# Order of the 64x64 products of a recurrence on TensorE: one half of the rows after the other, or the two halves in turn

## The chip, the cores and the metric

The kernel runs on one core of one Trainium2 chip. The metric is the device time of one execution in microseconds (us), lower is better. The kernel before was executed three times for its time; the median is 2512.82 us (2508.73 to 2514.59).

## The reference, cut to what matters

The reference is one layer of a decoder trunk: 256 tokens, 2048 channels, everything in float32. It has a token mixer of four parallel branches, a cross-attention into 256 memory tokens and a gated MLP. The change touches only one branch of the mixer, the RWKV-7 recurrence over 8 heads of 64 channels:

```python
def step(state, inp):
    r_t, w_t, k_t, v_t, kk_t, a_t = inp
    sa = jnp.einsum('bhvk,bhk->bhv', state, -kk_t)
    state = (state * w_t[:, :, None, :]
             + sa[..., None] * (kk_t * a_t)[:, :, None, :]
             + v_t[..., None] * k_t[:, :, None, :])
    return state, jnp.einsum('bhvk,bhk->bhv', state, r_t)
```

The projections around it (`z = h @ w_in` and the others) are large products of 128x128 weight tiles with 256 tokens.

## The kernel before, in words

**The recurrence in chunks.** The 256 steps are cut into 4 chunks of 64 tokens. In a chunk the recurrence becomes a set of 64x64 matrices per head: products of the scaled operands (the stages `rw_s1` to `rw_s4`), the inverse of a triangular matrix by five doubling levels (`rw_level`, `rw_level2`), and then, chunk by chunk, the right-hand side, the solution, the state and the output (`rw_chunk_a`, `_b`, `_c`).

**Where the matrices lie.** 8 heads by 4 chunks are 32 matrices of 64x64. Two heads share the 128 partitions: one head in partitions 0 to 63, the other in 64 to 127. So there are 16 positions `g` along the free axis, times 2 halves `h`. A product takes its two operands from one half of the partitions and writes its result to the same half of PSUM, so it uses 64 rows and 64 columns of TensorE's array: half 0 the one quarter, half 1 the quarter diagonally opposite.

**How a product becomes instructions.** Every float32 product of this kernel that isn't split by hand is two matmul instructions in the profile, each with a weight load of its own. A call of `pe.matmul` in these stages is thus two instructions on PE and two on PEld.

**The two helpers of the change.** `per_head` (L438) calls a product for all 16 positions of half 0 and then for all 16 of half 1: 32 products, 64 instructions. It is called 20 times (once in `rw_s1`, `rw_s2` and each of five `rw_level`; twice in `rw_s3`, `rw_s4` and in `rw_level2` of the levels 1 to 4; once in `rw_level2` of level 5). All these products are recorded under L452. In `rw_s1` and `rw_s2` a product has 128 columns, elsewhere 64. `four` (L525) does the same for the 4 positions of one chunk, where a result may be the sum of two or three products; its products are recorded under L531. It is called 15 times, for 224 products.

**PSUM.** `small_mm` puts position `g` at bank `base + g // 8` for 64 columns and `base + g // 4` for 128. `four` puts position `i` at bank `base + i // 2`.

**The order around it.** TensorE's queue is written out by hand: the list `MIX` holds the projections (`project`, L390, its matmuls under L396; those of the compressed keys under L615), and the dictionary `steps` (L742) says which recurrence stage is issued ahead of which projection. A projection is 16 products, or 32 instructions, and the burst of small products stands between two of them. VectorE and ScalarE evict the results of a burst (`rw_level`'s by L1671, which is `masked` at L1648, and L1673 and L1676) while TensorE does the next projection. The weights of a projection (1 MB) come through a ring of 4 slots, filled by SyncE (L326) once a slot has been used.

Of the kernel before, what the change touches and what calls it, by code (L numbers as in the profile page):

```python
# [139 lines left out]
def program(nc, A, const_dram, decay_dram, const_at, out):  # L140
# [4 lines left out]
    with ctx:  # L145
# [61 lines left out]
        sm = ctx.enter_context(nc.psum_tensor("sm", [P, 6, 512], f32))  # L207
# [174 lines left out]
        def _(pe):  # L382
# [55 lines left out]
            def per_head(fn):  # L438

                for h in range(2):
                    for g in range(16):
                        mm = fn(slice(64 * h, 64 * h + 64), g)
                return mm

            def b64(base, g, w=64):
# [42 lines left out]
            def rw_s1():  # L489
                pe.wait_ge(sem("rw_operands"), 1)  # L490
                pe.wait_ge(sem("rw_bonus_out"), 1)
                per_head(lambda r, g: small_mm(0, r, g, G["B"][r, g], QR[r, g, :, :], w=128)) \
                    .then_inc(sem("rw_s1_mm"), 1)

            def rw_s2():
                pe.wait_ge(sem("rw_s1_out"), 1)
                per_head(lambda r, g: small_mm(0, r, g, G["C"][r, g], QR[r, g, :, :], w=128)) \
                    .then_inc(sem("rw_s2_mm"), 1)

            def rw_s3():  # L500
                pe.wait_ge(sem("rw_s2_out"), 1)
                per_head(lambda r, g: small_mm(0, r, g, QR[r, g, 0, :], G["B"][r, g])).then_inc(sem("rw_s3_mm"), 1)
                per_head(lambda r, g: small_mm(2, r, g, G["Vc"][r, g], eye(r))).then_inc(sem("rw_s3_mm"), 1)
# [19 lines left out]
                        .then_inc(sem("rw_p2_mm"), 1)  # L523

            def four(base, off, fn):  # L525
                for h in range(2):
                    r = slice(64 * h, 64 * h + 64)
                    for i in range(4):
                        pairs = fn(r, i)
                        for q, (a, b) in enumerate(pairs):  # L530
                            mm = pe.matmul(sm[r, base + i // 2, off + i % 2 * 64:off + i % 2 * 64 + 64], a, b,  # L531
                                           start=q == 0, stop=q == len(pairs) - 1)
                return mm

            v4 = lambda a: a.rearrange("p (i t) -> p i t", t=64)
# [2 lines left out]
            def rw_chunk_a(c):  # L538

                if c == 0:  # L540
                    pe.wait_ge(sem("rw_x_ready"), 6)
                else:
                    pe.wait_ge(sem("rw_state"), c)
                    pe.wait_ge(sem("rw_y_out"), c)
                four(0, 0, lambda r, i: ([(QR[r, 4 * i + c, 0, :], S4[r, i])] if c else [])
                     + [(G["L2"][r, 4 * i + c], G["V"][r, 4 * i + c])]).then_inc(sem("rw_rhs_mm"), 1)

            def rw_chunk_b(c):

                pe.wait_ge(sem("rw_rhs_out"), c + 1)  # L550
                four(2, 0, lambda r, i: [(G["X"][r, 4 * i + c], X04[r, i])]).then_inc(sem("rw_u_mm"), 1)

            def rw_chunk_c(c):

                pe.wait_ge(sem("rw_u_out"), c + 1)
                if c < NCH - 1:
                    four(2, 128, lambda r, i: [(G["Bt"][r, 4 * i + c], U4[r, i]),
                                               (G["Ct"][r, 4 * i + c], G["V"][r, 4 * i + c])]) \
                        .then_inc(sem("rw_ds_mm"), 1)
                four(0, 128, lambda r, i: ([(S4[r, i], QR[r, 4 * i + c, 1, :])] if c else [])  # L560
                     + [(U4[r, i], G["M1"][r, 4 * i + c]), (G["V"][r, 4 * i + c], G["M2"][r, 4 * i + c])]) \
                    .then_inc(sem("rw_y_mm"), 1)
# [1587 lines left out]
```

## Time and profile before

| what | value |
|---|---|
| median of three executions | 2512.82 us |
| fastest, slowest | 2508.73, 2514.59 us |
| span of the profiled execution | 2503.8 us |
| median less span | 9.0 us |
| PE busy | 2398.1 us (96%), 14320 instructions |
| PEld busy | 2085.0 us (83%), 14320 instructions |
| DVE, ACT, POOL busy | 1384.9, 1045.6, 236.1 us |
| HBM read | 389.34 MB, 156 GB/s over the span |

The profile is one profiled execution. Its span runs from the first to the last recorded instruction; the listing has no separate total for it, so its own time is taken as the span and the 9.0 us that the median of the three executions lies above it. PE is TensorE's matmul, PEld its weight load, DVE is VectorE, ACT is ScalarE. The recorded duration of a matmul reaches from its start to a modelled end, and matmuls overlap in the pipeline, so the pace of a stream is read from its starts or from the length of the whole stream divided by its count, not from the mean duration.

### The profile page before, as it was taken

How to read it: one execution, taken by the hardware profiler on the slowest of the kernel's cores; microseconds unless marked ns; L12 is line 12 of the kernel's file. 1: busy time of each engine (PE TensorE's matmuls, PEld its weight loads, DVE VectorE, ACT ScalarE, POOL GpSimd, SP SyncE). 2: the span in 40 equal slices, each digit the busy share in tenths (PEclk: the TensorE clock that was granted, in tenths of full speed). 3: DMA queues.
4: the chain of work that ended last, by engine and by line, in shares of the span. 5: the costliest groups of instructions: out<-in, count | busy, mean ns of one | idle time of the engine just before them, and what ended most of it. 6: DMA issues, size and time to landing. Idle time of an engine off the chain costs nothing.

```text
span 2503.8 us, 38637 instructions
## 1 busy us (share of the span) xinstructions
PE 2398.1 (96%) x14320; PEld 2085.0 (83%) x14320; DVE 1384.9 (55%) x1676; ACT 1045.6 (42%) x1463; POOL 236.1 (9%) x240
## 2 busy tenths in 40 slices
PE   5989999999999999999999999896999999999996
PEld 4869989789888888887887888785888888888885
DVE  5661110221118666666677544356877777776665
ACT  4320001112114555555444444345655555555553
POOL 0120100000000000000421000031111111111110
PEclk9989997999999999999999999998999999999998
DMA  6512222233334555556555554252655555555663
GB/s 224 185 51 85 98 102 78 97 133 113 124 118 152 185 187 186 189 189 212 194 171 165 181 173 153 93 188 86 198 186 186 184 182 188 189 163 188 186 185 127
DMA packets 104459, 392.77 MB, mean 157 GB/s; under 512 B 11600, under 2 KB 20048, under 8 KB 94000
## 3 DMA queue, kind: packets, MB, share of 16 engines
q1 hardware_dynamic: 104080, 390.31, 47.2%
q8 instruction: 67, 1.10, 0.2%
q10 hardware_dynamic: 288, 1.17, 0.1%
q14 instruction: 24, 0.20, 0.0%
HBM read 389.34 MB, written 2.10 MB: 156 GB/s over the span
## 4 chain that ended last, share of the span: by engine, by line
PE 73%; issue 18%; DVE 6%; ACT 1%; POOL 1%; DMA 0%; DVEq 0%; POOLq 0%; ACTq 0%
PE bank L797 29%; PE bank L800 15%; PE bank L396 13%; PE sm L452 3%; PE bank L414 2%; PE bank L426 2%; PE sm L531 1%; PE bank L417 1%; PE bank L615 1%; DVE part L1876 1%; DVE part L1970 1%; DVE part L1539 1%; PE sm L905 1%; PE sm L435 1%; PE sm L887 1%
## 5 line engine op out<-in xcount | busy, mean ns | idle before, releaser
L797 PE MATMUL bank<-part,part 128*128 128x512 f32 x4224 | 1488.4, 399 | 35.1 <-issue 16.3
L800 PE MATMUL bank<-part,part 128*128 128x256 f32 x4224 | 1150.6, 282 | 0.0
L1876 DVE TENSOR_TENSOR part<-part,part 128x1024 fp32r<-128x1024 f32 (+1 forms) x632 | 795.0, 1268 | 370.7 <-ACT part L1139 358.4
L797 PEld LDWEIGHTS bank<-part,part 128*128 128x128 f32 x4224 | 783.8, 189 | 212.0 <-issue 20.1
L800 PEld LDWEIGHTS bank<-part,part 128*128 128x128 f32 x4224 | 799.7, 189 | 21.5
L1139 ACT ACTIVATE part<-part 128x1024 fp32r<-128x1024 f32 (+1 forms) x632 | 662.8, 1050 | 349.7 <-PE bank L800 320.9
L396 PE MATMUL bank<-part,part 128*128 128x256 f32 (+1 forms) x1632 | 364.3, 383 | 0.0
L396 PEld LDWEIGHTS bank<-part,part 128*128 128x128 f32 (+1 forms) x1632 | 307.4, 190 | 50.0 <-issue 5.1
L1213 ACT ACTIVATE part<-bank 128x256 f32<-128x256 f32 x236 | 90.3, 382 | 291.1 <-PE bank L797 291.1
L992 ACT ACTIVATE part<-bank 128x256 f32<-128x256 f32 (+1 forms) x59 | 22.7, 384 | 413.3 <-PE bank L396 375.5
L1884 DVE TENSOR_TENSOR part<-bank,part 128x256 f32<-128x256 f32 (+1 forms) x236 | 99.8, 423 | 132.9 <-ACT part L1213 132.8
L1476 POOL TENSOR_TENSOR part<-part 128x256 f32 (+1 forms) x48 | 48.1, 1003 | 763.2 <-DVE part L1884 763.2
L797 PE MATMUL sm<-part,part 128*128 128x512 f32 x320 | 110.8, 397 | 1.3 <-DVE part L1890 0.7
L414 PE MATMUL bank<-part,part 128*128 128x512 f32 x256 | 90.9, 403 | 8.7 <-DVE part L1575 8.7
L800 PE MATMUL sm<-part,part 128*128 128x256 f32 x320 | 79.4, 281 | 0.0
L452 PEld LDWEIGHTS sm<-part 64*64 64x64 f32 x1088 | 71.6, 139 | 7.6 <-issue 7.6
L452 PE MATMUL sm<-part 64*64 64x64 f32 (+1 forms) x1088 | 73.7, 233 | 2.1 <-DVE part L1639 2.1
L1501 POOL TENSOR_TENSOR part<-part 128x256 f32<-128x256 f32 x44 | 32.5, 738 | 424.1 <-DVE part L2051 424.1
L417 PE MATMUL bank<-part,part 128*128 128x256 f32 x256 | 69.8, 283 | 0.0
L797 PEld LDWEIGHTS sm<-part,part 128*128 128x128 f32 x320 | 56.8, 188 | 11.0 <-DVE part L1890 1.5
L800 PEld LDWEIGHTS sm<-part,part 128*128 128x128 f32 x320 | 60.1, 188 | 5.8
L414 PEld LDWEIGHTS bank<-part,part 128*128 128x128 f32 x256 | 47.7, 190 | 20.4 <-issue 9.7
(304 smaller groups left out, 1576.0 us busy)
## 6 DMA issues: line engine op xcount, KB each, us to landing
part<-in_w_up SPq DMA_DIRECT2D x176, 512.0 KB, 4.5
part<-in_w_g SPq DMA_DIRECT2D x104, 512.0 KB, 4.2
part<-in_w_dn SPq DMA_DIRECT2D x64, 512.0 KB, 3.5
part<-in_w_out SPq DMA_DIRECT2D x32, 512.0 KB, 4.0
part<-in_w_mk SPq DMA_DIRECT2D x32, 512.0 KB, 4.3
part<-in_w_mv SPq DMA_DIRECT2D x32, 512.0 KB, 3.9
part<-in_w_q SPq DMA_DIRECT2D x32, 512.0 KB, 3.8
part<-in_w_o SPq DMA_DIRECT2D x32, 512.0 KB, 3.9
```

The lines of the kernel that those rows point to most:

```text
L396: mm = pe.matmul(big[0:M, n % 2, 0:rhs_n], w[:, k * M:(k + 1) * M], x[:, k, :], start=k == 0, stop=k == KT - 1)
L414: mm = pe.matmul(b, w[:, 0, k, :], x, start=h == 0 and k == 0, stop=last, skip_group_check=True)
L417: mm = pe.matmul(b[:, T:2 * T], w[:, 1, k, :], x[:, 0:T], start=False, stop=False, skip_group_check=True)
L426: mm = pe.matmul(dst[:, s * P:(s + 1) * P], x[:, k, s * P:(s + 1) * P], ring[:, n % NSLOT, k, :], start=k == 0, stop=k == KT - 1)
L452: return pe.matmul(sm[rows, b, c:c + w], lhsT, rhs, start=start, stop=stop)
L797: mm = pe.matmul(dst, w[:, 0, k, :], x[:, k0 + k, :], start=start and k == 0, stop=last, skip_group_check=True)
L800: mm = pe.matmul(dst[:, T:2 * T], w[:, 1, k, :], x[:, k0 + k, 0:T], start=False, stop=False, skip_group_check=True)
L1139: act.activation(wsplit[(2 * m + h) % 4][:, 0, 0:n, :], raw[:, m % 2, h, 0:n, :], cp) .then_inc(sem("hi_done"), 1)
L1213: act.activation(cross[:, b, :], bank[:, b, T:2 * T], cp).then_inc(sem("cross_out"), 1)
L1476: pool.tensor_tensor(sq[:, n % 2:n % 2 + 1, :], tile, tile, MUL).then_inc(sem("y_sq"), 1)
L1876: tt(w[:, 1, 0:n, :], raw[:, m % 2, h, 0:n, :], w[:, 0, 0:n, :].bitcast(f32), SUB).then_inc(sem("lo_done"), 1)
L1884: tt(dst, bank[:, b:b + 1, 0:T], cross[:, b:b + 1, :], ADD).then_inc(sem("prod_out"), 1)
```

## The change

In `per_head` the two loops change places, so that a product of half 0 is followed by one of half 1; half 1 takes its positions turned by 8, `(g + 8 * h) % 16`, so that two neighbours in the order never write to the same PSUM bank. In `four` the loop over the halves goes innermost, inside the sum over pairs, and half 1 takes its positions turned by 2. The number of instructions, their shapes, the waits and the signals stay as they are; the signal still hangs on the last product of the call.

```diff
             def per_head(fn):
-                for h in range(2):
-                    for g in range(16):
-                        mm = fn(slice(64 * h, 64 * h + 64), g)
+                for g in range(16):
+                    for h in range(2):
+                        mm = fn(slice(64 * h, 64 * h + 64), (g + 8 * h) % 16)
                 return mm
...
             def four(base, off, fn):
-                for h in range(2):
-                    r = slice(64 * h, 64 * h + 64)
-                    for i in range(4):
-                        pairs = fn(r, i)
-                        for q, (a, b) in enumerate(pairs):
-                            mm = pe.matmul(sm[r, base + i // 2, off + i % 2 * 64:off + i % 2 * 64 + 64], a, b,
-                                           start=q == 0, stop=q == len(pairs) - 1)
+                rows = [slice(64 * h, 64 * h + 64) for h in range(2)]
+                for i in range(4):
+                    at = [(i + 2 * h) % 4 for h in range(2)]
+                    pairs = [fn(rows[h], at[h]) for h in range(2)]
+                    for q in range(len(pairs[0])):
+                        for h in range(2):
+                            a, b = pairs[h][q]
+                            c = off + at[h] % 2 * 64
+                            mm = pe.matmul(sm[rows[h], base + at[h] // 2, c:c + 64], a, b,
+                                           start=q == 0, stop=q == len(pairs[h]) - 1)
                 return mm
```

## Rows read from the trace of the kernel before

**Rows 1.** Stretches of the mixer: us; PE, PEld, DVE, ACT, POOL busy; granted clock; DMA.
```profile
170.30:182.30 12.00, 11.97 (x65) 11.67 (x65) 0.00 (x0) 0.00 (x0) 0.00 (x0) 0.55 0.00 1
182.30:190.80 8.50, 8.50 (x34) 7.01 (x33) 4.80 (x4) 0.00 (x0) 0.00 (x0) 0.83 0.00 0
...
197.60:350.00 152.40, 152.40 (x1548) 138.02 (x1549) 27.45 (x36) 6.66 (x14) 16.76 (x21) 1.00 0.24 89
371.10:377.10 6.00, 6.00 (x66) 5.88 (x65) 0.00 (x0) 0.20 (x2) 0.00 (x0) 0.50 0.50 175
377.10:400.50 23.40, 23.40 (x153) 22.25 (x153) 1.27 (x3) 3.36 (x9) 0.00 (x0) 0.65 0.25 90
400.50:408.20 7.70, 7.70 (x82) 7.58 (x81) 0.00 (x0) 0.20 (x1) 0.76 (x2) 0.50 0.39 138
```

**Rows 2.** All waits of PE from 170.5 to 479.7 us: total, times, longest.
```profile
PE sm L452 <- DVE part L1639: 2.1, 1, 2.1
PE sm L588 <- ACT part L992: 0.5, 1, 0.5
```

**Rows 3.** Groups of PE from 170 to 480 us, the small products, shapes kept apart.
```profile
L452 PE MATMUL sm<-part 64*64 64x64 f32 x960 | 54.9, 220 | 0.0
L531 PE MATMUL sm<-part 64*64 64x64 f32 x448 | 31.4, 251 | 0.0
...
L452 PE MATMUL sm<-part 64*64 64x128 f32 x128 | 18.8, 333 | 2.1 <-DVE part L1639 2.1
L452 PE MATMUL sm<-cst,part 64*64 64x64 f32 x192 | 10.9, 220 | 0.0
```

**Rows 4.** Chain that ended last, 165 to 480 us: start, us, what.
```profile
170.33 11.98 PE sm L452 x64
...
190.84 6.75 PE sm L452 x64
...
204.69 7.07 PE sm L452 x128
...
233.03 3.69 PE sm L452 x64
...
356.23 0.89 PE sm L531 x16
...
371.14 5.92 PE sm L531 x64
...
387.14 1.83 PE sm L531 x32
...
400.55 7.62 PE sm L531 x80
...
435.38 4.27 PE sm L531 x80
...
469.75 2.76 PE sm L531 x48
```

**Rows 5.** Instructions of PE in time where rw_s3 passes from half 1 to half 0.
```profile
207.00 1.21 PE L452 MATMUL sm<-part 64*64 64x64 f32 x18
208.00 0.27 PE L452 MATMUL sm<-cst,part 64*64 64x64 f32 x1
208.05 0.22 PE L452 MATMUL sm<-part 64*64 64x64 f32 x1
208.10 0.22 PE L452 MATMUL sm<-cst,part 64*64 64x64 f32 x1
208.11 0.22 PE L452 MATMUL sm<-part 64*64 64x64 f32 x1
...
208.22 0.57 PE L452 MATMUL sm<-cst,part 64*64 64x64 f32 x7
```

**Rows 6.** The costliest group of DVE from 204 to 350 us.
```profile
L1648 DVE TENSOR_TENSOR part<-sm,cst 128x1024 f32<-128x1024 f32 x5 | 6.1, 1225 | 45.4 <-PE sm L452 45.4
```

**Rows 7.** DMA issues from 165 to 480 us: KB each, median us from issue to landing.
```profile
part<-in_w_cmp SPq DMA_DIRECT2D x4, 1024.0 KB, 4.9
```

## The prediction

> **What bounds the kernel now.** I read the page first: PE is busy for 96% of the span, so the question is whether the touched stage is PE's too. The chain of waits from 165 to 480 us answers it: it runs through PE's small products and the projections between them, with nothing of another engine in between worth a microsecond (one burst of each length stands in [rows 4]). The waits of PE say the same: from 170.5 us to 479.7 us it waited 2.6 us in all [rows 2]. So a microsecond that a burst gives back is a microsecond off the end, unless the projection behind it then waits.
>
> The groups give the size of the work: 960 + 192 + 128 instructions under L452 and 448 under L531 [rows 3], together 1728, for 864 products. The chain has them in 26 bursts: six of 128 instructions at 7.07 us, six of 64 at 3.69, one of 64 at 11.98 (rw_s1) and one at 6.75 (rw_s2), five of 16 at about 0.9, three of 32 at 1.83, one of 64 at 5.92, one of 80 at 7.62, one of 80 at 4.27, one of 48 at 2.76 [rows 4]. That is 114 us, the most that the change could touch.
>
> **The pace.** 18 instructions in a row take 1.21 us with 0.22 for the last alone [rows 5]: (1.21 - 0.22) / 17 = 0.058 us from start to start. The six steps among the seven later ones give (0.57 - 0.22) / 6 = 0.058 too. The granted clock there is 1.00, the 2.4 GHz level (the stretch from 197.6 us in [rows 1]).
>
> The view that decides is the order of time where rw_s3 goes from half 1 (sm<-part) to half 0 (sm<-cst,part). The starts are 207.99 (the last of the 18), 208.00, 208.05, 208.10, 208.11, then two at 208.16 (one of each kind), 208.22 [rows 5]. The two halves start **side by side**: each keeps its own steps of 0.058 us and does not see the other. A hand-over saves three starts, 3 x 0.058 = 0.17 us. With k hand-overs a burst of N then takes (N - 3k) x 0.058 plus a fixed piece; the exact pace that fits is 0.0583. For 64 and k = 1: 61 x 0.0583 = 3.56, fixed piece 0.13. For 128 and k = 3: 119 x 0.0583 + 0.13 = 7.07, as measured. 16, 32, 80 and 48 give 0.89, 1.82, 4.27 and 2.75: all match [rows 4]. So the overlap is there at every change of half and at no other place, and the change makes every product a change of half.
>
> **The change, part by part.** It adds and removes no instruction, wait, signal or DMA. It moves products inside a call only, so nothing passes another engine's queue, and the signal stays on the last product.
>
> If the halves run side by side throughout, each burst takes N / 2 x p + 0.13 us:
> - 128: 64 x 0.0583 + 0.13 = 3.86, saves 3.21, six times: 19.3
> - 64: 2.00, saves 1.69, six times: 10.1
> - 16: 0.60, saves 0.29, five times: 1.5; 32: 1.06, saves 0.77, three times: 2.3
> - 80 at 4.27: 2.46, saves 1.8; 48: 1.53, saves 1.2
> - the 64 at 5.92 and the 80 at 7.62 run at granted clock 0.50, the 1.2 GHz level [rows 1]; p = (5.92 - 0.13) / 55 = 0.105: they take 3.5 and 4.3, saving 2.4 and 3.3
> - rw_s2 (128 columns): p = 6.62 / 61 = 0.1085, takes 3.6, saves 3.15
> - rw_s1: clock 0.55 [rows 1], p = 11.85 / 61 = 0.194, takes 6.35, saves 5.6
>
> Sum 50.6 us.
>
> **What covers the rest.** The evictions between two bursts are hidden by a projection of 7.1 us (182.3 to 190.8 us, 8.5, at clock 0.83 [rows 1]). A DVE pass over a whole stage is 1.225 us and DVE sat 45.4 us idle before five of them [rows 6]; at most three stand between two bursts, 3.7 us. The projection doesn't shrink, so the cover stays; without it a level would cost those 3.7 us. A weight chunk needs 4.9 us to land [rows 7] and is asked for three chunks ahead; a projection and its burst will take 9 to 11 us in place of 11 to 14, so the ring keeps up. I take both at nothing; a late chunk would cost at most 4.9 us.
>
> **The clock.** It is the unsure part of the sum. Around rw_s1 and in the stretch from 371 us the granted clock is 0.50 to 0.65 [rows 1]. The projection behind rw_s1 takes 8.5 us for its 7.1. Denser bursts leave less slow time behind, or the thin products between them fill more of it. One projection of 7.1 us at 1.2 GHz instead of 2.4 costs 7.1 us more, and one freed gives as much back. I take zero for it and put 7 to 8 us to both sides of the likeliest case.
>
> **The unknown cost: how fast instructions reach the array in the new order.** The trace shows 8 starts in 0.23 us (0.029 each), but only across a boundary, with three starts of each half beside one another; no row has it for longer. The bounds are 0.029 (the halves never wait for the queue) and 0.058 (the queue is what sets today's pace, and the overlap lives from instructions stored ahead). I take 0.029, nearest to the row that shows the two halves together; against 0.058 stands that the pace at the half clock is 0.105, so the array sets it and not the queue. The Trainium skill (TensorE: Matmul & The Clock Gate, Back-to-back issue gap) gives a floor of about 25 ns from start to start however small the product. By it 29 ns is just allowed and the sum stays; were each weight load to take such a slot as well, a pair would cost 50 ns, which is a result inside the first rival below.
>
> **Rivals.**
>
> 1. *The queue becomes the bound.* At 0.044 us per instruction, midway, the 22 bursts at full clock with 64 columns (1456 instructions, 81.6 us now) take 1456 x 0.044 + 22 x 0.13 = 66.9, saving 14.7; the four others are above that pace anyway and save 14.4. Total 29 us: 2484. At 0.058 the 22 bursts lose their hand-overs (87.3 us, 6 worse), the others save some 13.5, together 7 to 8 us: 2505. For it: nothing shows the pace for longer than a hand-over. Against it: hand-overs after short runs are as full as after long ones (k = 3 fits for 128).
>
> 2. *Slower: each return to a half loads its weights in the open.* The first instruction of a new half is followed by its second after 0.10 us, not 0.058 (208.00 and 208.10 in [rows 5]); 0.044 us more. If products then don't overlap (one half must end before the other may begin), each of the 864 pays it: 38 us, and the 44 hand-overs of today (0.17 each) are lost, 7.5 us. Time 2512.8 + 45.5 = 2558. It decides from the point where the mean start to start in a full-clock burst is above today's 81.6 / 1456 = 0.056 us. Against it: with the same extra load, but the halves side by side, two products take 0.16 us where now they take 0.23, and the trace shows them side by side.
>
> 3. *No change to be measured.* The array takes the new order as today's, pace for pace, or the freed time is handed back as half clock. The first needs a rule that allows overlap at a boundary and not within; the second needs 50 us more of loss to the clock, where the slow part from 371 to 408 us is only about 30 us long (6.0, 0.7 x 23.4 at a mean of 0.65, 7.7 [rows 1]). 2508 to 2518.
>
> **How the numbers follow.** The profiled execution's span is 2503.8 us and the median of the runs 9.0 above it; minus 50.6 gives a span of 2453.2 and a time of 2462 us. About 0.2%, 5 us, can be told from no change here. Chances: side by side throughout 0.76, time 2454 to 2470 (the clock's 7 to 8 us both ways); queue-bound 0.13, 2470 to 2505; no change 0.05; slower 0.06, around 2558. The range for 8 in 10 takes the likeliest case and the queue-bound one to its middle: 2454 to 2486. Faster by over 0.2%: 0.76 + 0.13 = 0.89; within: 0.05; slower: 0.06.
>
> **What the profile after would show.** Right: the same 1728 instructions; in the order of time starts in couples or evenly 0.029 apart; bursts of 128 at 3.9 us and of 64 at 2.0 in the chain, rw_s1 near 6.4; DVE idle shorter before L1648 by as much; PE's waits still 2 to 3 us from 170 us on. Rival 1: an even pace between 0.03 and 0.058, with PE reported idle on nothing. Rival 2: steps of 0.10 and 0.058 in turn, bursts longer than now. Wrong in the cover: waits of L452 or L531 for DVE or ACT, or of L396 for a DMA. Wrong in the clock: the same bursts, but other slow stretches between 350 and 480 us, or in later stages, which the change doesn't touch.

## The result and the profile after

The changed kernel takes 2455.45 us in the median of four executions (2449.19 to 2456.19). Beside it the kernel before took 2510.78. The ratio is 0.9772, with a 95% interval of 0.9755 to 0.9789, so the change is worth 57 us (53 to 61.5) of about 2511. The forecast was 2462 us, 50.6 us less than before. The sign and the mechanism are as forecast, but the sum of the steps lies below the interval of the gain. By the ratio (0.9772 x 2510.78 = 2453.5) the time falls 0.5 us under the low end of the range, 2454. Two things bring it there: some 6 us more were gained than the bursts explain, and the kernel before stands at 2510.78 here and stood at 2512.82 in the forecast. The experiments went after the 6 us.

The profiled execution of the changed kernel took 2449.19 us with a span of 2447.4, so only 1.8 us lie outside the span. Its chain of waits, the pieces that answer to [rows 4] (start, us, what):

```profile
170.11 6.17 PE sm L452 x64
176.28 7.10 PE bank L396 x32
183.38 3.64 PE sm L452 x64
...
194.12 3.88 PE sm L452 x128
...
216.09 2.01 PE sm L452 x64
...
316.44 0.61 PE sm L534 x16
...
331.10 3.61 PE sm L534 x64
334.71 4.13 PE bank L618 x32
338.85 3.28 PE sm L599 x8
342.13 1.23 PE sm L534 x32
...
353.13 3.84 PE sm L534 x80
...
382.03 2.48 PE sm L534 x80
...
411.89 1.54 PE sm L534 x48
...
420.54 1.72 PE sm L570 x4
```

L534 is `four`, L531 before; L618 is the projection of the compressed keys, L615 before. The burst of 128 has gone from 7.07 to 3.88 us, the one of 64 from 3.69 to 2.01, and the projection between them is 7.10 as it was. The last line is the first step behind the recurrence (`rw_mean`). In the chain of the kernel before, that step and two projections that matter below are

```profile
377.06 6.96 PE bank L615 x32
...
461.07 8.68 PE bank L396 x32
...
479.61 1.72 PE sm L567 x4
```

So 59.1 us are gained by then, of which 0.2 lie ahead of rw_s1. All 26 bursts together, read from the two chains, give 50.8 us, where the forecast had 50.6. The rest of the kernel gives 2.7 back: from rw_mean to the end it is 2024.2 us before and 2026.9 after.

The small products as groups, against [rows 3], and the waits of PE from 170.5 to 420.5 us, against [rows 2]:

```profile
L452 PE MATMUL sm<-part 64*64 64x64 f32 x960 | 30.4, 219 | 0.0
L534 PE MATMUL sm<-part 64*64 64x64 f32 x448 | 18.8, 247 | 0.0
...
L452 PE MATMUL sm<-part 64*64 64x128 f32 x128 | 9.9, 325 | 2.8 <-DVE part L1642 2.8
...
L452 PE MATMUL sm<-cst,part 64*64 64x64 f32 x192 | 6.0, 219 | 0.0
```
```profile
PE sm L452 <- DVE part L1642: 2.8, 1, 2.8
PE sm L591 <- ACT part L995: 0.5, 1, 0.5
```

The counts are the same, the busy times about half, and the mean duration of one product is unchanged (219 against 220 ns): a single product is no faster, two of them run at once. No wait has come in behind a burst, so the cover held. The granted clock is where the surplus shows. Stretches of the changed kernel, columns as in [rows 1]:

```profile
170.10:176.20 6.10, 6.09 (x64) 5.93 (x64) 0.00 (x0) 0.00 (x0) 0.00 (x0) 0.58 0.01 3
176.30:183.40 7.10, 7.10 (x34) 5.99 (x36) 4.80 (x4) 0.00 (x0) 0.00 (x0) 1.00 0.00 0
...
334.70:353.10 18.40, 18.40 (x156) 17.05 (x154) 1.27 (x3) 3.37 (x9) 0.00 (x0) 0.78 0.34 127
353.10:357.00 3.90, 3.90 (x82) 3.83 (x81) 0.00 (x0) 0.20 (x1) 0.76 (x2) 0.62 0.71 246
```

The projection behind rw_s1 runs at 1.00 (0.83 before), the stretch with the thin products at 0.78 (0.65 before), the burst of 80 at 0.62 (0.50 before). The projections run the same instructions as before, and so the change reached them through the clock alone. Between 300 us and rw_mean the records of the granted clock in the two traces add up to 37.5 us at the 1.2 GHz level before and 17.1 after.

### The profile page after: what moved, and what is told of

Its sections match the earlier page's. It is cut to its first block, busy times and chain, and to the rows that moved or that the text cites. A ratio compares the mean times of both kernels' runs of the same rounds, so it can differ in the third digit from the quotient of the medians.

```text
span 2447.4 us, 38637 instructions
## 1 busy us (share of the span) xinstructions
PE 2343.7 (96%) x14320; PEld 2030.6 (83%) x14320; DVE 1384.5 (57%) x1676; ACT 1045.3 (43%) x1463; POOL 236.0 (10%) x240
## 4 chain that ended last, share of the span: by engine, by line
PE 73%; issue 19%; DVE 6%; ACT 1%; POOL 1%; DMA 0%; DVEq 0%; POOLq 0%; ACTq 0%
PE bank L800 30%; PE bank L803 15%; PE bank L396 13%; PE bank L414 2%; PE bank L426 2%; PE sm L452 2%; PE bank L417 1%; DVE part L1879 1%; PE bank L618 1%; PE sm L534 1%; DVE part L1973 1%; PE sm L908 1%; DVE part L1542 1%; PE sm L435 1%; PE sm L890 1%
## 5 line engine op out<-in xcount | busy, mean ns | idle before, releaser
L800 PEld LDWEIGHTS bank<-part,part 128*128 128x128 f32 x4224 | 785.0, 189 | 212.0 <-issue 20.1
L803 PEld LDWEIGHTS bank<-part,part 128*128 128x128 f32 x4224 | 800.9, 190 | 21.5
L414 PEld LDWEIGHTS bank<-part,part 128*128 128x128 f32 x256 | 47.9, 191 | 20.2 <-issue 9.4
L1389 ACT ACTIVATE part<-part,vec 128x256 f32<-128x256 f32 x88 | 52.6, 597 | 17.6 <-DVE part L2048 13.2
L426 PEld LDWEIGHTS bank<-part,part 128*128 128x128 f32 x512 | 58.1, 192 | 1.9 <-issue 1.9
```

The lines of the kernel that those rows point to most:

```text
L414: mm = pe.matmul(b, w[:, 0, k, :], x, start=h == 0 and k == 0, stop=last, skip_group_check=True)
L426: mm = pe.matmul(dst[:, s * P:(s + 1) * P], x[:, k, s * P:(s + 1) * P], ring[:, n % NSLOT, k, :], start=k == 0, stop=k == KT - 1)
L800: mm = pe.matmul(dst, w[:, 0, k, :], x[:, k0 + k, :], start=start and k == 0, stop=last, skip_group_check=True)
L803: mm = pe.matmul(dst[:, T:2 * T], w[:, 1, k, :], x[:, k0 + k, 0:T], start=False, stop=False, skip_group_check=True)
L1389: act.activation(ub[:, p % 2, s, :], rawu[:, s, :], ACT.Identity, bias=col(b0), scale=col(w2)) \
```

## The experiments

**The changed kernel again** (no edit).

> The changed kernel again, to size the part of the gain that the bursts do not explain. In the first comparison the sum of the bursts was 50.6 us and the ratio of the runs 0.977, which is 57 us. Theory A (the burst terms are right, and a further 5 to 8 us come from the clock, because thin products and slow projections get shorter slow stretches between 320 and 360 us): ratio 0.9765 to 0.979, bursts of 128 at 3.88 us and of 64 at 2.01, slow time between 320 and 420 us again near 17 us, not the 37 us of before. Theory B (the 5 us are scatter of the clock in later stages that the change does not touch): ratio 0.979 to 0.981, and the slow time of the mixer differs from look to look.

Ratio 0.9774 (0.9761 to 0.9786), and the bursts at 3.88 and 2.01 us. rw_mean starts at 419.85 us. The surplus came back, in the mixer and of the same size, so it is no scatter from one execution to the next. That it is of the clock this run alone can't say.

**Each helper alone.** e1 has the new `per_head` and the old `four`; e2 has the old `per_head` and the new `four`. The code of both is that of the change's diff.

> Only per_head alternates, four is as before. Theory A: the 14 bursts of L452 give 19.3 + 10.1 + 3.1 + 5.6 = 38 us, and 1 to 2 more from the projection behind rw_s1 that runs at the full clock; the bursts of four keep their 0.89, 1.83, 5.92 and 7.62 us, and the slow stretches around them return to about 37 us. Ratio near 0.984. Theory B (no tie between the order of four and the slow stretches): 38 us and no more, ratio 0.985, the slow time between 320 and 420 us anywhere between 17 and 37 us.

> Only four alternates, per_head is as before. Theory A: its 12 bursts give 1.5 + 2.3 + 1.8 + 1.2 + 2.4 + 3.3 = 12.5 us, and the shorter slow stretch around the thin products 5 to 7 us more: 18 to 20 us, ratio 0.992 to 0.993. Theory B: 12.5 us and no more, ratio 0.995.

e1 measured 0.9847 (0.9835 to 0.9860), 38.4 us, where its bursts were to give 38; a surplus of 0 and one of 3 us both fit. e2 measured 0.9924 (0.9912 to 0.9937), 19 us, where its bursts were to give 12.5; here a surplus is shown. The two add up to 57.4, the whole change.

The chains say where it lies. From the first projection of the thin products (the 30-column products of the compressed keys) to the end of the projection behind L604 (L607 after) it is 50.6 us before, 49.1 in e1, 38.6 in e2 and 38.6 in the changed kernel. The forecast for the bursts in there was 6.8 us. So 5.2 us of surplus in this stage come with `four`, and at most 1.5 with `per_head`. The 1.4 us of the projection behind rw_s1 come with `per_head`: it takes 7.11 us in e1 and 8.80 in e2. e1 first, then e2:

```profile
330.09 5.03 PE sm L531 x64
335.11 6.96 PE bank L615 x32
```

```profile
371.17 3.53 PE sm L534 x64
374.71 4.01 PE bank L618 x32
...
387.26 6.11 PE bank L618 x32
393.37 4.47 PE sm L534 x80
```

The second projection of 30-column products took 6.96 us before and in e1, and takes 4.01 here, without being touched.

**Only the banks, without the halves.**

```diff
                 for h in range(2):
                     for g in range(16):
-                        mm = fn(slice(64 * h, 64 * h + 64), g)
+                        mm = fn(slice(64 * h, 64 * h + 64), g % 2 * 8 + g // 2)
```

> per_head finishes one half first as before, but goes through its positions in the order 0, 8, 1, 9 and so on, so that neighbours write to two banks in turn; four is as before. It has the bank half of the change without the other half. Theory A (only the turn between row halves matters): bursts of 128 stay at 7.07 us and of 64 at 3.69, ratio 1.000 within 0.2%. Rival (the pace of 0.058 us against the 0.053 that 128 steps at 2.4 GHz would take is a price for staying in one bank): pace 0.053, the 1280 instructions save some 6 us, ratio 0.998.

1.0003 (0.9994 to 1.0012), and the bursts are those of the kernel before:

```profile
218.55 7.07 PE sm L452 x128
...
232.72 3.69 PE sm L452 x64
```

Going from bank to bank within one half does nothing.

**Only the halves, without the banks.**

```diff
-                        mm = fn(slice(64 * h, 64 * h + 64), (g + 8 * h) % 16)
+                        mm = fn(slice(64 * h, 64 * h + 64), g)
...
-                    at = [(i + 2 * h) % 4 for h in range(2)]
+                    at = [i for h in range(2)]
```

> The changed kernel without the turn of the positions: half 0 and half 1 take the same position one after the other, so the neighbours write to the same PSUM bank, in different partitions, in per_head and in four. Theory A (the halves are independent as long as their rows and their PSUM partitions differ): bursts of 128 at 3.9 us and of 64 at 2.0, ratio 0.977 as with the turn. Rival (two rows halves can't write to one bank at the same time): the halves take turns, bursts of 128 at about 7.2 us, ratio at or above 0.995.

0.9748 (0.9731 to 0.9765), against 0.9772 (0.9755 to 0.9789) for the change; the intervals overlap. In the chain of this kernel the bursts are those of the change:

```profile
204.02 3.88 PE sm L452 x128
...
215.00 2.01 PE sm L452 x64
```

Here two products write to one bank side by side, to different partitions of it, at the same pace as into two banks. The Trainium skill (TensorEngine Tiling (Array Packing), Gotcha 1: PSUM Pressure) says that different row tiles can't access the same PSUM bank at the same time. Here the tiles differ in their columns of the array too, and so in their partitions; for that case the measurement decides, and the turn of the positions is not needed for the time.

**Longer runs in one half.** `n` is 2 in e4 and 4 in e5; `four` is that of the change.

```diff
-                for g in range(16):
-                    for h in range(2):
-                        mm = fn(slice(64 * h, 64 * h + 64), (g + 8 * h) % 16)
+                for g0 in range(0, 16, n):
+                    for h in range(2):
+                        for g in range(g0, g0 + n):
+                            mm = fn(slice(64 * h, 64 * h + 64), (g + 8 * h) % 16)
```

> per_head changes the half after every 2 products (4 instructions) and not after every one; four as in the change. Theory A (at a change of half the three or four instructions next in line run beside the other half's): with 4 instructions per run the overlap is still complete, bursts of 128 at 3.9 us and of 64 at 2.0, ratio 0.977 to 0.979. Rival (the overlap costs something at each change, so that longer runs are better or worse): another length.

> per_head changes the half after every 4 products (8 instructions); four as in the change. Theory A (a hand-over saves three starts and no more): a burst of 64 has 7 hand-overs, (64 - 21) x 0.0583 + 0.13 = 2.64 us, a burst of 128 has 15, (128 - 45) x 0.0583 + 0.13 = 4.97 us; against the change these lose 6 x 1.1 + 6 x 0.6 + rw_s2 1.2 + rw_s1 2.1 = 13.5 us, ratio 0.9825. Rival (the array works ahead as far as it is given products, the trace of before only had too few changes to show it): 3.9 and 2.0 us, ratio 0.977.

e4: 0.9766 (0.9750 to 0.9782). e5: 0.9788 (0.9769 to 0.9806). The chains of the two, e4 first:

```profile
194.75 3.93 PE sm L453 x128
...
216.81 2.06 PE sm L453 x64
```
```profile
184.48 4.47 PE sm L453 x64
196.06 4.92 PE sm L453 x128
...
220.10 2.62 PE sm L453 x64
```

Its profiled execution, the slowest of its four (2453.4 to 2464.6 us), has a span of 2462.8, 15 us above that of the change; 11.6 of them are the longer bursts, the rest is slow clock. The bursts carry the verdict; the time doesn't show it by itself.

**TensorE kept busy ahead of rw_s1.**

```diff
             def rw_bonus():
+                for j in range(27):
+                    pe.matmul(sm[:, 5, 0:T], cc("ones128"), hT[:, j % KT, :], start=True, stop=True)
                 pe.wait_ge(sem("rw_g_out"), 1)
...
             def rw_s1():
+                for j in range(21):
+                    pe.matmul(sm[:, 5, 0:T], cc("ones128"), hT[:, j % KT, :], start=True, stop=True)
                 pe.wait_ge(sem("rw_operands"), 1)
```

> The changed kernel with products that nobody reads (128x256, into a bank that is free there) in the two idle times of TensorE ahead of rw_bonus and rw_s1, 27 and 21 of them. Theory A (the slow clock around rw_s1 follows from TensorE's idle time there): the granted clock stays at 1.00, rw_s1 takes twice less, 3.64 us like rw_s2 and not 6.17, and the end comes 2.5 us sooner, ratio 0.976. Rival (the 64x64 products themselves bring the clock down): rw_s1 stays at 6.2 us, ratio 0.977.

0.9801 (0.9786 to 0.9816), slower than the change by some 7 us. I had sized the filler wrongly: a product of 256 columns is two instructions of 0.216 us and not of 0.107, as the chain shows:

```profile
156.54 11.65 PE sm L484 x54
168.19 1.72 PE sm L488 x4
169.91 9.07 PE sm L493 x42
178.97 3.64 PE sm L452 x64
```

The filler put rw_s1 off by 8.9 us. But rw_s1 itself takes 3.64 us in place of 6.17, exactly as rw_s2: here the small products don't bring the clock down, the idle time ahead of them did. The 2.5 us that rw_s1 gives back were forecast rightly; the sooner end was not, since the filler cost more.

**The thin products widened.**

```diff
+                    at = 30 * (16 * kv + k)
+                    cols = min(120, 960 - at)
-                    mm = pe.matmul(big[:, n % 2, 0:30], ring[:, n % NSLOT, k, :],
-                                   blk[:, kv, k].rearrange("p g c -> p (g c)"), start=k == 0, stop=k == 15)
+                    mm = pe.matmul(big[:, n % 2, 0:cols], ring[:, n % NSLOT, k, :],
+                                   slab(26640, 960)[:, at:at + cols], start=k == 0, stop=k == 15)
```

e8 is the changed kernel with this edit, e12 (its label is e12b) the kernel before with it.

> The changed kernel with the products of the compressed keys (128x30) widened to 120 columns, of which 90 are read by nobody; a weight load of 128 columns paces them either way. Theory A (the slow stretches between 320 and 360 us come from the 30-column products, and are shorter in the changed kernel because less slow work lies beside them): no slow stretch is left there; the four projections take 3.7 us each and not 4.7, 4.1, 3.7 and 5.5, the bursts of 64 and 80 2.0 and 2.5 and not 3.6 and 3.8, the products of L599 1.9 and not 3.3; about 8 us in all, ratio 0.974. Rival (they come with the bursts or the waits): the slow stretches stay and the time stays at 0.977.

> The kernel before with the 120-column products alone. Theory A (in the kernel before, 34 us of half clock between 369 and 411 us come from the 30-column products; the change gained its 6 to 8 us beyond the bursts because less of the work lies there): the slow stretches go, and the bursts of 64 and 80 take 3.7 and 4.3 us; 15 to 17 us in all, ratio 0.9935. The changed kernel with the same products stood at 0.9734, so with the clock out of the way the change would be worth 0.9734 / 0.9935 = 0.980, 50 us, the sum of the bursts. Theory B (the surplus is not of the clock): ratio 0.996 (as the widening brought the changed kernel 8 to 10 us), and the change still worth 57 us on top.

e8: 0.9734 (0.9721 to 0.9747). e12: 0.9926 (0.9910 to 0.9942), 18.5 us (14.5 to 22.5) from an edit that makes the products four times wider. The stretch of 50.6 us from above takes 35.0 in its chain, 15.6 less and within the 15 to 17 that were expected; rw_s1 and the projection behind it, where the slow clock falls otherwise, take 1.8 back. The stretch with the thin products, e8 first, then e12, columns as in [rows 1]:

```profile
326.00:358.00 32.00, 32.00 (x398) 29.66 (x398) 4.52 (x9) 5.46 (x16) 0.76 (x2) 1.00 0.45 164
```
```profile
366.00:410.00 44.00, 43.64 (x443) 40.50 (x444) 4.53 (x9) 7.17 (x18) 0.75 (x2) 1.00 0.35 125
```

The clock is 1.00 in both, where [rows 1] shows 0.50 to 0.65 and the changed kernel 0.62 to 0.78. The chain of e12 shows what that does to work that the edit doesn't touch, the burst of 80 at 4.27 in place of 7.62 us:

```profile
375.48 3.76 PE bank L617 x32
...
387.38 3.69 PE bank L617 x32
391.07 4.27 PE sm L531 x80
```

With this slow stretch out of the way on both sides, the change is worth 0.9734 / 0.9926 = 0.981, about 48 us (within 5), and no longer 57. The profiles say it more closely: from the start of rw_s1 to rw_mean it is 295.5 us in e12 and 244.7 in e8, 50.8 us. Of these, 6.6 are rw_s1 (13.1 against 6.5) and 2.1 the projection behind it. The other 42.1 stand against 42.4 by the formula (the 45.0 of the forecast without rw_s1, less 5.7 for the two bursts at half clock, plus 3.1 for the same two at full clock). The 5.2 us of surplus in the stage with the thin products are gone once nothing brings the clock down there: that part is shown to be of the clock, by taking its cause away. What is left over the forecast, 2.1 us of the projection and 1.0 of rw_s1, lies in the slow stretch around rw_s1, which the edit doesn't touch.

One slow stretch stays in both, and nothing here explains it: the projection ahead of the burst of 48. It takes 8.68 us before, 6.99 in the changed kernel (twice), but 8.68 again in e8,

```profile
397.65 8.68 PE bank L396 x32
```

and 8.68 in e2 and e3 too, with the bursts of `four` as in the change. So the change doesn't set it, and its 1.7 us in the comparison of the two profiles are not shown to be a gain of the change.

**Stages one projection later.** In e10 all stages from `rw_bonus` on move from `("sc", 3)` on to the next key, on TensorE and on ScalarE:

```diff
-                ("sc", 0): [rw_lora], ("sc", 1): [rw_g], ("sc", 3): [rw_bonus, rw_s1],
-                ("sc", 4): [rw_s2], ("sc", 5): [rw_s3], ("sc", 6): [rw_s4],
+                ("sc", 0): [rw_lora], ("sc", 1): [rw_g], ("sc", 4): [rw_bonus, rw_s1],
+                ("sc", 5): [rw_s2], ("sc", 6): [rw_s3], ("sc", 7): [rw_s4],
...
```

> The changed kernel with every recurrence stage from rw_bonus on issued one projection later, on TensorE and ScalarE, so that a projection of 7.1 us stands where TensorE now waits 5.9 us for VectorE ahead of rw_bonus. Theory: those 5.9 us, and the slow time behind them (rw_s1 6.17 to 3.64 us), 8 us in all, ratio 0.974; the 2.8 us ahead of rw_s1 stay. Rival (the later stages now stand ahead of other projections and wait there): up to 5 us of new waits in front of rw_chunk_b or nsa_rot_kc, ratio 0.976 to 0.977.

0.9765 (0.9749 to 0.9780): the rival. The 5.9 us ahead of rw_bonus are down to 0.7, but the waits of PE in this kernel are

```profile
PE sm L682 <- DVE part L1799: 4.7, 1, 4.7
PE sm L452 <- DVE part L1643: 3.9, 1, 3.9
PE sm L486 <- DVE part L1636: 0.7, 1, 0.7
```

The first is new, and not where I had looked for it: VectorE's norms of the recurrence end later against TensorE's projections, so the scaled probabilities of the sparse attention come late (L1799), and L682, which transposes them, waits 4.7 us. rw_s1 starts only 0.6 us sooner, since VectorE's chain sets its start whatever TensorE does meanwhile.

**The candidate.** e8 with the stages moved, but `rw_chunk_a(0)`, `nsa_rot_k` and `rw_chunk_b(0)` in one place at `("cmp", 0)`, so that everything from `rw_chunk_c(0)` on stands where the change has it.

```diff
-                ("kv", 5): [lambda: rw_chunk_a(0)],
-                ("cmp", 0): [nsa_rot_k, lambda: rw_chunk_b(0)], ("cmp", 1): [lambda: rw_chunk_c(0)],
+                ("kv", 4): [lambda: rw_level(5)], ("kv", 5): [lambda: rw_level2(5)],
+                ("cmp", 0): [lambda: rw_chunk_a(0), nsa_rot_k, lambda: rw_chunk_b(0)], ("cmp", 1): [lambda: rw_chunk_c(0)],
```

> A candidate that should beat both kernels: the changed kernel with the 120-column products of e8, and with the stages from rw_bonus to rw_level2 of level 5 one projection later; rw_chunk_a(0) and rw_chunk_b(0) then share one place, so that from rw_chunk_c(0) on the order is the changed kernel's again and VectorE's norms are not late as in e10. Theory: against e8 (0.9734) TensorE's wait of 5.9 us ahead of rw_bonus is filled, and nothing waits later: ratio 0.971. Rival (the wait turns up at another place, as it did in e10): ratio 0.973 to 0.974, with a wait of some us for VectorE or ScalarE between 300 and 460 us.

0.9692 (0.9676 to 0.9708), 2431.56 us: it beats both kernels, the changed one by about 20 us. PE's only wait from 150 to 470 us is the one ahead of rw_s1:

```profile
PE sm L452 <- DVE part L1643: 3.5, 1, 3.5
```

Against e8 that is some 10 us (5 to 16), where 5.9 were expected (0.971). The chains show what the forecast left out. A whole projection of 7.1 us now stands ahead of rw_s1, which starts at 170.14 us as before: besides the wait of 5.6 it fills time that the slow clock took behind it (L486 lasts 1.88 us for 3.75 in e8). The wait of 0.5 us for ScalarE ahead of the thin products is gone. And the projection ahead of the burst of 48 takes 6.99 us here, not 8.68, which is the unexplained 1.7 us again.

## Why the prediction was right in its mechanism and short in its sum

**That the halves run side by side throughout: right.** rw_s3's start in the changed kernel, in order of time, is

```profile
194.05 0.62 PE L452 MATMUL sm<-part 64*64 64x64 f32 x14
```

14 instructions, (0.62 - 0.22) / 13 = 0.031 us from start to start, with the first weight loads among them. The single starts in the trace come in couples, 0.007 us apart, each couple 0.058 behind the one before; over the whole burst it is 3.88 / 128 = 0.030, where one half alone goes at 0.058. The forecast said 3.86 and 2.00 us for 128 and 64, measured are 3.88 and 2.01; 0.60, 1.53 and 2.46 became 0.61, 1.54 and 2.48; rw_s2 3.6 became 3.64, rw_s1 6.35 became 6.17. (That rw_s1 is so near is partly luck: with the same products it takes between 5.38 and 6.48 us in the repeat, e1, e3 and e8, as the slow clock falls on it.) The reading of one place in the trace of before, the hand-over of [rows 5], was enough for this, and e5 shows that the formula drawn from it holds at a third spacing of the hand-overs as well.

**Rival 1, the queue as the next bound: wrong.** No pace between 0.03 and 0.058 is seen in the full-clock bursts of the changed kernel, once the fixed piece of 0.13 us is taken off. The Trainium skill's floor of about 25 ns from start to start (TensorE: Matmul & The Clock Gate, Back-to-back issue gap) is not contradicted by the mean of 30 ns; that it doesn't hold between the two halves is shown by [rows 5], where starts follow each other by 0.01 us.

**Rival 2, weights loaded in the open at each return: wrong.** Only the start of a burst pays the 0.10 us, once for both halves: the first couple of starts in rw_s3 is at 194.06 us, the second at 194.16, and from there on the step is 0.058.

**Cover: right.** VectorE has 37.1 us of idle time left ahead of the five passes of [rows 6] (45.4 before), and no projection waits:

```profile
L1651 DVE TENSOR_TENSOR part<-sm,cst 128x1024 f32<-128x1024 f32 x5 | 6.1, 1224 | 37.1 <-PE sm L452 37.1
```

**The step that failed: "I take zero for it", of the clock.** The term measured 8 us in the mixer. From the chains, pieces with the same instructions in the same order: the projection behind rw_s1 8.53 to 7.10, the second and fourth projection of thin products 6.96 to 4.13 and 6.96 to 5.47, L604 (L607 after) 2.00 to 1.09 and the projection at 461 us 8.68 to 6.99. That is 8.4 us, less 0.5 for the first thin projection and L596, which became slower. The 1.7 of the projection at 461 us are in it, and they don't follow the change, as e2, e3 and e8 show. The later stages gave 2.7 back, in a profile whose 11037 instructions there kept PE busy 1960.8 us for 1957.9; behind 500 us the time at the 1.2 GHz level went from 57.7 to 62.4 us, and half of that difference, 2.4, is my estimate of the cost.

Which way the clock would go is shown by the runs. In the stage with the thin products it stands at the 1.2 GHz level for 30.7 to 34.1 us with the old `four` (before, e1, e6), for 13.7 to 20.5 us with the new one (the change and its repeat, e2, e3, e4, e5, e7, e10), and not at all with 120 columns (e8, e12, the candidate). I had named both directions and weighed them alike. Why it goes this way isn't shown. The less time a slow stretch has, the less work is caught in it; but it may also be that the denser bursts let the clock rise sooner. Before, it stays down through the burst of 64 and for 9.5 us behind it; after, it is back 0.9 us behind that burst. No run here tells the two apart.

**A second, smaller error: the base.** The 9.0 us between the span of before and the median were taken as what lies around the span. That piece is 1.8 us. The other 7.2 are that the profiled execution of before was a quick one, quicker than all three shown (2503.8 + 1.8 = 2505.6 against 2508.73 at best). It drops out of the difference, since the forecast takes 50.6 from the median either way. The median itself matters for the range: with 2512.82 for the kernel before, the same ratio gives 2455.5 us, inside it. The two profiles differ by 56.4 us, the medians by 55.3 and the ratio gives 57, and none of these should be read to the last microsecond.

## What to carry to other kernels

Two streams of 64x64 products in opposite quarters of the array (rows and columns both apart) ran at twice the pace of one here, and the order of issue was all that was needed: change the quarter after every one or two products, since after every four (e5) part of the overlap is gone. Look for a place in the trace where the order changes quarter by accident; its starts tell what the reorder would bring, without an experiment. And where thin products stand between dense ones, look at the granted clock of all that follows them: widening them from 30 to 120 columns left a projection of them at 3.7 to 3.8 us and was worth 18 us in one kernel and some 10 in the other.

## What was not expected of the hardware

- The bank plays no part: same bank (e3) or alternating banks in one half (e6) change no burst at full clock by more than 0.01 us.
- Matmuls don't start in the order in which they are issued, when they belong to different halves. In [rows 5] the first of the next call start ahead of the last ones of the call before.
- The overlap reaches only a few instructions across a change of half: three starts per hand-over with runs of 8, 16 and 32 instructions, complete overlap with runs of 2 and 4.
- The granted clock fell to the 1.2 GHz level while TensorE was 100% busy with 30-column products, and stayed at 2.4 GHz with 120 columns, with the same count of products and 3.7 to 3.8 us per projection, which the 30-column products take too where the clock is high (3.69).
